# Encoder step on one core: in the first projection, each term's weight tiles start 64 bytes further on than the term's before

## The chip, the cores and the metric

The kernel runs on one core of one Trainium2 chip. Its time is the device time of one execution in microseconds (us); three executions of the kernel before are at hand, and the times of two kernels are compared by their medians. Five engines run their own instruction streams side by side: TensorE (PE in the profile, with its weight loads shown apart as PEld), VectorE (DVE), ScalarE (ACT), GpSimd (POOL) and SyncE (SP, which only issues transfers here).

## The reference

One inference step of a two-layer hybrid encoder, with 2048 prompt tokens and 8 x 16 sample tokens (2176 in all), model width 1024. What matters here is the first line of each layer, the input projection:

```python
def in_proj(x, g, w):
    p = rmsnorm(x, g) @ w
    m = MIX_WIDTH
    return (p[..., :m], p[..., m:2 * m], p[..., 2 * m:3 * m],
            heads(p[..., 3 * m:3 * m + X_WIDTH], H_X, HD_X), p[..., 3 * m + X_WIDTH:])
```

It is a product of a 2176 x 1024 matrix of tokens with a 1024 x 3584 matrix of weights, once for each layer. Layer 0 then does banded softmax attention, layer 1 a gated linear recurrence; both also do a small cross-attention, a gate and an output projection. All tensors are float32.

## The kernel before

The span falls into stages: a short beginning (function `begin`), the first projection (`project` with `l = 0`, from 50.5 us to about 657 us of the profiled execution), banded attention with its output projection (to about 1337 us), the second projection (`project` with `l = 1`, to 1964 us), and the recurrence.

**Seven terms.** A projection is a product of 2 x 2 blocks done with seven block products in place of eight (Strassen's scheme). A pair of 128-column weight groups gives, with its two halves of the 1024 rows, four blocks; `Terms.SUMS` and `Terms.PLAIN` say which sum, difference or plain block is the weight of term j, j = 0 to 6. `Halves` does the same for the tokens. There are 14 pairs (`WPAIRS`), so one pass over all weights has 98 steps (`STEPS`, one step for one term of one pair), and there are four passes (`PASSES`), each over a quarter of the tokens: 320 token columns a term in the first pass (the sample tokens ride along), 256 in the other three. A projection is 392 steps.

**Three products a step.** Each float32 operand is split into a high part in `float32r` and a low part (what the high part leaves out). One step of TensorE is, for each of four 128-row pieces k, three matmuls: weights high with tokens high, weights low with tokens high, weights high with tokens low. That is 12 matmuls a step, each with its own load of a 128 x 128 weight tile. In TensorE's loop:

```python
for i, (a, y) in enumerate(((w.hi, x.hi), (w.lo, x.hi), (w.hi, x.lo))):
    ins = nc.tensor.matmul(BANK[j][:, 0:n], a[j][:, k], x.of(y, p, j)[:, k],
                           start=(k == 0 and i == 0), stop=(k == 3 and i == 2))
```

**Where a term's weights come from.** In the first pass the sums are made from raw weights and kept in DRAM (`tsum`). In the later passes SyncE fetches a term of 256 KB into `pj0_wt` (`Terms.fetch`, once the term's matmuls of seven steps ago are done), ScalarE makes `pj0_wh` from it (`Terms.high`), and VectorE makes `pj0_wl` (`Terms.low`), which lies in the same bytes as `pj0_wt`. TensorE waits for `pj0_wl`. ScalarE and VectorE also take the seven products out of PSUM and combine them into `pj0_out`. Every program order is written out by hand, as loops over the step number `t`; a semaphore count stands for each tile.

**Where the tiles lie.** Tiles are placed one behind the other in each partition of SBUF, in the order in which the code asks for them. By the built program's table of addresses (bytes within a partition): the token tiles `x0_hi` and `x0_lo` of slots 0 to 6 start at 42464 and every 5120 bytes after it, those of slots 7 and 8 at 26080 and every 4096 bytes. A piece k of a token tile is 1280 bytes after the one before it in the first pass, 1024 in the later ones. The weights start at 151072, behind a spacer of 64 bytes (`pj0_shift`): a term is `wh` (2048 bytes) and `wl` (2048 bytes), and its pieces k are 512 bytes apart. So every weight piece that TensorE loads in passes two to four lies 64 bytes above a multiple of 512 bytes away from every token piece. In the first pass a piece k of the tokens is 1280 k bytes on, so that the same figure, the distance modulo 512, is 64 for even k and 320 for odd k. In the second projection, spacers (`pj1_shift0`, `pj1_pad1`, `pj1_shift1`) hold the same 64. In the output projections, the stationary operand is the gated activations and the moving one 512 columns of weights; there the distance modulo 512 is 0 in the odd-numbered jobs of the attention stage, 160 in its even-numbered jobs, and 288 in the recurrence.

What the change touches is `Terms.term`, which places a term's three tiles; it is called in `hybrid_encoder` for j = 0 to 6 of each layer.

Of the kernel before, what the change touches and what calls it, by code (L numbers as in the profile page):

```python
# [20 lines left out]
P = 128  # L21
# [364 lines left out]
class Terms:  # L386
# [22 lines left out]

    def term(self, j, sb, shadowed):  # L410
        l = self.l
        self.hi[j] = sb(f"pj{l}_wh{j}", [P, 4, P], F32R)
        with ExitStack() as shadow:
            self.sum[j] = shadowed(shadow)(f"pj{l}_wt{j}", [P, 4, P])
        self.lo[j] = sb(f"pj{l}_wl{j}", [P, 4, P], F32R)
# [518 lines left out]
def project(nc, l, sem, ps_in, v, x, w, x_of, proj, keep, room, early, samp, opening):  # L934
# [59 lines left out]
    with ExitStack() as ctx:  # L994
# [45 lines left out]
        with nc.Block() as block:  # L1040
# [123 lines left out]
            def _(act):  # L1164
# [56 lines left out]
                for t in range(ALL + 2 * TERMS):  # L1221
# [17 lines left out]
                    if p < PASSES - 1:  # L1239
                        if c in (1, 3, 5, 7) and j == 1:  # L1240
                            square(4 * p + c // 2)
                        if c in (2, 4, 6, 8) and j == 3:
                            evacuate(4 * p + c // 2 - 1, 0)
                        if c in (3, 5, 7, 9) and j == 0:
                            evacuate(4 * p + c // 2 - 1, 1)
                        if (c, j) in ((9, 6), (10, 2)):
                            x.high(nc, act, p + 1, c - 9)
                        for at, term in ((2, 2), (3, 3), (4, 4), (5, 5), (6, 6)):
                            if (c, j) == (WPAIRS - 1, at):
                                act.wait_ge(s_mm, STEPS * (p + 1) - TERMS + term - 1)  # L1250
                                x.high(nc, act, p + 1, term)
# [4 lines left out]
            def _(dve):  # L1256
# [71 lines left out]
                for t in range(ALL + 2 * TERMS):  # L1328
# [20 lines left out]
                    if p < PASSES - 1:  # L1349
                        i = 4 * p + c // 2  # L1350
                        if c in (1, 3, 5, 7) and j == 3:
                            dve.wait_ge(s_sq, i + 1)
                            nc.vector.tensor_scalar(ms[:, i:i + 1], ss[:, i:i + 1], 1.0 / D, EPS, ALU.mult, ALU.add).then_inc(s_ms, 1)
                        if c in (1, 3, 5, 7) and j == 6:
                            dve.wait_ge(s_rs, i + 1)
                            nc.vector.tensor_scalar(nat[i % 2][:], nat[i % 2][:], rs[:, i:i + 1], None, ALU.mult).then_inc(s_xn, 1)
                        for at, term in (((9, 4), 0), ((10, 0), 6), ((10, 5), 2), ((11, 5), 5), ((12, 1), 4)):
                            if (c, j) == at:
                                dve.wait_ge(x.s_raw, RAWS + 8 * (p + 1))
                                if l == 0 and p == 0 and term == 0:  # L1360
                                    dve.wait_ge(keep.s_out, 128)
                                    dve.wait_ge(keep.s_row, 16)
                                x.add(nc, dve, p + 1, term)
                        for at, term in (((10, 2), 0), ((11, 1), 1)):
                            if (c, j) == at:
                                x.low(nc, dve, p + 1, term)
                        for at, term in ((3, 2), (4, 3), (5, 4), (6, 5)):
                            if (c, j) == (WPAIRS - 1, at):
                                x.low(nc, dve, p + 1, term)
# [1973 lines left out]
```

## Time and profile before

| | us |
|---|---|
| median of 3 runs | 2460.17 |
| lowest, highest | 2459.54, 2461.45 |
| the profiled execution's own time | 2456.59 |
| its span, first to last instruction | 2454.8 |
| of that, the first projection's matmuls | 50.5 to 657.1 |

The profiled execution is 3.6 us below the median, and 1.8 us of its own time lies around the span. A row of a view by groups gives, for one line, engine and pair of tiles, the count, the busy time, the mean duration and the idle time before it with what ended it. The distance between the starts of neighbouring matmuls is their price when they are pipelined; the duration of one (some 276 ns) is longer, as it overlaps the next ones.

### The profile page before, as it was taken

The numbers are of one execution on the slowest core, as the hardware profiler recorded it, in microseconds if no ns is written. First come the engines' busy times: TensorE is split into PE (matmuls) and PEld (weight loads), VectorE is DVE, ScalarE is ACT, GpSimd is POOL, SyncE is SP. The second block draws the span as 40 slices with busy tenths as digits, with TensorE's granted clock in tenths as the row PEclk, the third lists the DMA queues.
The fourth block names the chain that finished last, engine by engine and source line by source line (L and its number), as shares of the span: only waits on it lengthen the run. The fifth ranks groups of instructions, "written<-read, shape, count | busy, mean of one in ns | idle before, by whom it ended". The sixth has DMA issues, their size and how long they took to land. (4 is left out here: it accounts for less than half of the span.)

```text
span 2454.8 us, 61024 instructions
## 1 busy us (share of the span) xinstructions
PE 2368.7 (96%) x23677; PEld 2082.7 (85%) x23677; DVE 1852.3 (75%) x3597; ACT 1451.1 (59%) x3323; POOL 372.9 (15%) x585
## 2 busy tenths in 40 slices
PE   7999999999999999999998999999999979999998
PEld 5999999999866777777776899999999978888886
DVE  7899788887665555555555999888898867888885
ACT  4655667755565555454554565676766656666664
POOL 2332000000022111111111332000000031212211
PEclk9999999999999999999999999999999989999999
DMA  6887888889883222222223888888789794344441
GB/s 234 291 288 260 290 284 250 246 260 296 249 261 92 81 79 70 72 76 79 71 78 136 276 291 278 254 264 241 243 253 299 259 285 120 119 139 124 133 139 68
DMA packets 402706, 480.59 MB, mean 196 GB/s; under 512 B 40532, under 2 KB 249228, under 8 KB 402424
## 3 DMA queue, kind: packets, MB, share of 16 engines
q1 hardware_dynamic: 385880, 417.03, 54.5%
q0 software_dynamic: 14704, 54.92, 6.6%
q10 hardware_dynamic: 1840, 4.75, 0.7%
q8 instruction: 192, 3.15, 0.5%
q14 instruction: 90, 0.74, 0.1%
HBM read 329.78 MB, written 151.56 MB: 196 GB/s over the span
## 5 line engine op out<-in xcount | busy, mean ns | idle before, releaser
L1428 PE MATMUL pj_acc<-x_hi,pj_wh 128*128 128x256 f32 (+1 forms) x3080 | 888.9, 289 | 26.4 <-DVE pj_wl L483 23.6
L1428 PE MATMUL pj_acc<-x_hi,pj_wl 128*128 128x256 f32 (+1 forms) x3080 | 876.8, 285 | 0.0
L1428 PE MATMUL pj_acc<-x_lo,pj_wh 128*128 128x256 f32 (+1 forms) x3080 | 876.7, 285 | 0.0
L476 ACT ACTIVATE pj_wh<-pj_wt 128x512 fp32r<-128x512 f32 x718 | 449.8, 634 | 351.5 <-DMA pj_wt<-tsum 245.9
L1428 PEld LDWEIGHTS pj_acc<-x_hi,pj_wh 128*128 128x128 f32 x3080 | 579.0, 188 | 40.2 <-DVE pj_wl L483 37.7
L483 DVE SCALAR_TENSOR_TENSOR pj_wl<-pj_wt,pj_wh 128x512 fp32r<-128x512 f32 x718 | 498.6, 710 | 110.9 <-ACT pj_wh L476 98.9
L1428 PEld LDWEIGHTS pj_acc<-x_lo,pj_wh 128*128 128x128 f32 x3080 | 579.8, 188 | 0.0
L1428 PEld LDWEIGHTS pj_acc<-x_hi,pj_wl 128*128 128x128 f32 x3080 | 579.0, 188 | 0.1
L1275 DVE TENSOR_TENSOR pj_out<-pj_out,pj_acc 128x512 f32<-128x512 f32 (+1 forms) x448 | 320.2, 715 | 66.2 <-PE pj_acc L1428 39.3
L2553 ACT COPY pb_pt<-pb_TP 128x384 f32<-128x384 f32 (+2 forms) x272 | 107.0, 393 | 288.6 <-PE pb_TP L2268 219.4
L2437 DVE COPY pb_pt<-pb_TP 128x256 f32<-128x256 f32 (+2 forms) x266 | 115.8, 435 | 139.8 <-PE pb_TP L2265 130.9
L2420 DVE CUSTOM_DVE_ANT_0 pb_se<-pb_SC,pb_bias 128x640 f32<-128x640 f32 (+4 forms) x204 | 147.9, 725 | 82.4 <-PE pb_SC L2241 75.9
L2265 PE MATMUL pb_TP<-ident,pb_se 128*128 128x128 f32 x1020 | 170.4, 287 | 4.6 <-DVE pb_v L2457 2.7
L2546 ACT ACTIVATE pb_se<-pb_se,pb_mn 128x640 f32<-128x640 f32 (+4 forms) x208 | 156.9, 754 | 8.0 <-DVE pb_mn L2420 3.0
L2265 PEld LDWEIGHTS pb_TP<-ident,pb_se 128*128 128x128 f32 x1020 | 107.2, 140 | 54.5 <-issue 39.7
L2241 PEld LDWEIGHTS pb_SC<-pb_k,pb_q 64*128 64x128 f32 x1128 | 91.1, 186 | 42.2 <-issue 36.6
L2364 PE MATMUL pb_OP<-pb_woh,pb_yh 128*128 128x512 f32 x272 | 119.9, 441 | 2.1 <-DVE pb_x L2487 2.1
L2319 PEld LDWEIGHTS pb_OB<-pb_pt,pb_v 128*64 128x64 f32 x1680 | 89.8, 136 | 34.9 <-ACT pb_pt L2553 26.1
L2241 PE MATMUL pb_SC<-pb_k,pb_q 64*128 64x256 f32 (+1 forms) x1128 | 117.6, 340 | 1.6 <-issue 1.6
L2364 PE MATMUL pb_OP<-pb_woh,pb_yl 128*128 128x512 f32 x272 | 118.5, 436 | 0.0
L2895 PE MATMUL hg_OP<-woh,hg_yh 128*128 128x512 f32 x264 | 116.3, 440 | 0.0
L1175 ACT COPY pj_out<-pj_acc 128x256 f32<-128x256 f32 (+1 forms) x224 | 85.3, 381 | 49.1 <-PE pj_acc L1428 45.8
(354 smaller groups left out, 3922.5 us busy)
## 6 DMA issues: line engine op xcount, KB each, us to landing
pj_wt<-tsum SPq DMA_DIRECT2D x588, 256.0 KB, 3.7
proj<-pj_out SPq DMA_DIRECT2D x112, 512.0 KB, 4.3
tsum<-pj_wt SPq DMA_DIRECT2D x140, 256.0 KB, 3.3
pj_wraw<-in_w_in_dram POOLq DMA_DIRECT2D x24, 1024.0 KB, 7.0
tsum<-pj_wraw SPq DMA_DIRECT2D x56, 256.0 KB, 3.8
hg_x<-x_mid SPq DMA_DIRECT2D x17, 512.0 KB, 3.6
pb_gate<-proj SPq DMA_DIRECT2D x16, 512.0 KB, 5.0
pb_x<-in_x_prompt_dram SPq DMA_DIRECT2D x16, 512.0 KB, 3.5
```

Of the source, the lines that this page charges most:

```text
L476: nc.scalar.mul(self.hi[j][:], self.source(step), scale_of(c, self.l)).then_inc(self.s_hi, 1)
L483: nc.vector.scalar_tensor_tensor(out=self.lo[j][:], in0=self.source(step), scalar=scale_of(c, self.l), in1=self.hi[j][:].bitcast(F32), op0 ...
L1275: nc.vector.tensor_tensor(to, to, what, op).then_inc(s_cb, 1)
L1428: ins = nc.tensor.matmul(BANK[j][:, 0:n], a[j][:, k], x.of(y, p, j)[:, k], start=(k == 0 and i == 0), stop=(k == 3 and i == 2))
L2241: ins = nc.tensor.matmul(SC[h][:, at * P:(at + size) * P], q[T % 2][po:po + HD, p], kring[po:po + HD, p, slot * P:(slot + size) * P], star ...
L2265: ins = nc.tensor.transpose(TP[:, at:at + P], se[u % 2][h][:, i * P:(i + 1) * P], ident[:])
L2364: ins = nc.tensor.matmul(OP[:], (yl if part == 2 else yh)[job % 2][:, k], (wol if part == 1 else woh)[:, group_of(job, k), cs], start=(k = ...
L2420: nc.vector.tensor_tensor_reduce(se[u % 2][h][:, 0:n * P], SC[h][:, 0:n * P], add, 1.0, 3e38, ALU.add, ALU.min, mn[:, at:at + 1]).then_inc ...
L2437: ins = nc.vector.tensor_copy(pt[h][:, low * P:low * P + width], TP[:, 512:512 + width])
L2546: nc.scalar.activation(se[u % 2][h][:, 0:n], src[:, 0:n], ACT.Exp, bias=mn[:, at:at + 1], scale=-1.0, accum_out=tot[:, at:at + 1]).then_in ...
L2553: nc.scalar.copy(pt[h][:, 0:at], TP[:, 0:at]).then_inc(s_eva, 1)
L2895: nc.tensor.matmul(to[:], yh[:, s], woh[:, g, cs], start=(s == 0), stop=False)
```

## The change

One call is added: in the first projection, ahead of the tiles of each term but the first, 16 float32 values (64 bytes in a partition) are left free. Nothing reads or writes them.

```diff
     def term(self, j, sb, shadowed):
         l = self.l
+        if l == 0 and j:
+            sb(f"pj{l}_step{j}", [P, 16])
         self.hi[j] = sb(f"pj{l}_wh{j}", [P, 4, P], F32R)
```

By the two built programs, the instructions of every engine, their order and the semaphores that they wait for are the same; the line numbers behind the edit grow by 2. What differs is the addresses. The tiles of term j lie 64 j bytes further on (`pj0_wh1` 64, `pj0_wh6` 384), and what lies behind them, 384 bytes: the beginning's buffers and `pj0_nat`, `pj0_out`, `pj0_sig`. The distance of term j's weight pieces from the token pieces, modulo 512, becomes 64 (j + 1): 64, 128, 192, 256, 320, 384, 448 in passes two to four. In the first pass it is that for even k, and for odd k 256 bytes on from it (modulo 512): 320, 384, 448, 0, 64, 128, 192. The second projection and the other stages keep their addresses.

## Rows read from the trace of the kernel before

**Rows 1.** The page: busy time by engine, and the costliest groups.

```profile
PE 2368.7 (96%) x23677; PEld 2082.7 (85%) x23677; DVE 1852.3 (75%) x3597; ACT 1451.1 (59%) x3323; POOL 372.9 (15%) x585
...
L1428 PE MATMUL pj_acc<-x_hi,pj_wh 128*128 128x256 f32 (+1 forms) x3080 | 888.9, 289 | 26.4 <-DVE pj_wl L483 23.6
L1428 PE MATMUL pj_acc<-x_hi,pj_wl 128*128 128x256 f32 (+1 forms) x3080 | 876.8, 285 | 0.0
```

**Rows 2.** Busy time and clock in the first projection's four passes, all engines.

```profile
core 0: us, PE busy (x) PEld busy (x) DVE busy (x) ACT busy (x) POOL busy (x), PEclk, DMA share, GB/s
50.50:232.40 181.90, 179.74 (x1208) 177.69 (x1209) 161.40 (x214) 97.82 (x191) 63.32 (x50) 0.99 0.84 279
232.40:374.50 142.10, 140.11 (x1210) 138.41 (x1209) 117.38 (x183) 95.54 (x197) 4.44 (x8) 1.00 0.88 283
374.50:512.70 138.20, 137.51 (x1210) 137.11 (x1209) 117.07 (x183) 96.16 (x196) 7.33 (x7) 1.00 0.80 248
512.70:657.10 144.40, 139.36 (x1178) 137.06 (x1176) 104.33 (x165) 77.27 (x147) 0.00 (x0) 1.00 0.90 270
```

**Rows 3.** Who PE waited for from 50 to 657 us: us, times, longest.

```profile
PE pj_acc L1428 <- DVE pj_wl L483: 8.9, 17, 1.2
```

**Rows 4.** PE in the timeline, from 534 us (fourth pass): start us, duration.

```profile
534.27 0.28 PE L1428 MATMUL pj_acc<-x_lo,pj_wh 128*128 128x256 f32 x1
534.38 0.28 PE L1428 MATMUL pj_acc<-x_hi,pj_wh 128*128 128x256 f32 x1
...
542.43 0.28 PE L1428 MATMUL pj_acc<-x_lo,pj_wh 128*128 128x256 f32 x1
```

**Rows 5.** The same from 617 us (fourth pass).

```profile
617.39 0.28 PE L1428 MATMUL pj_acc<-x_lo,pj_wh 128*128 128x256 f32 x1
617.51 0.28 PE L1428 MATMUL pj_acc<-x_hi,pj_wh 128*128 128x256 f32 x1
...
627.28 0.28 PE L1428 MATMUL pj_acc<-x_lo,pj_wh 128*128 128x256 f32 x1
```

**Rows 6.** Matmuls by group in passes two, three, four, and 542.6 to 570.9 us.

```profile
L1428 PE MATMUL pj_acc<-x_lo,pj_wh 128*128 128x256 f32 x392 | 108.5, 277 | 0.0
...
L1428 PE MATMUL pj_acc<-x_lo,pj_wh 128*128 128x256 f32 x393 | 108.5, 276 | 0.0
...
L1428 PE MATMUL pj_acc<-x_lo,pj_wh 128*128 128x256 f32 x393 | 109.5, 279 | 0.0
...
L1428 PE MATMUL pj_acc<-x_hi,pj_wh 128*128 128x256 f32 x77 | 21.7, 282 | 1.1 <-DVE pj_wl L483 1.1
```

**Rows 7.** First pass: three matmuls at the lower clock, four at the higher.

```profile
53.31 0.47 PE L1428 MATMUL pj_acc<-x_hi,pj_wl 128*128 128x320 f32 x1
53.58 0.47 PE L1428 MATMUL pj_acc<-x_lo,pj_wh 128*128 128x320 f32 x1
...
57.43 0.31 PE L1428 MATMUL pj_acc<-x_hi,pj_wh 128*128 128x320 f32 x1
57.58 0.31 PE L1428 MATMUL pj_acc<-x_hi,pj_wl 128*128 128x320 f32 x1
57.73 0.31 PE L1428 MATMUL pj_acc<-x_lo,pj_wh 128*128 128x320 f32 x1
57.87 0.31 PE L1428 MATMUL pj_acc<-x_hi,pj_wh 128*128 128x320 f32 x1
```

**Rows 8.** Output projections in the timeline: distance 160, 288 and 0, in this order.

```profile
1332.78 0.39 PE L2364 MATMUL pb_OP<-pb_woh,pb_yl 128*128 128x512 f32 x1
...
1334.18 0.39 PE L2364 MATMUL pb_OP<-pb_woh,pb_yl 128*128 128x512 f32 x1
...
2439.77 0.40 PE L2895 MATMUL hg_SC<-woh,hg_yh 128*128 128x512 f32 x1
...
2441.17 0.40 PE L2895 MATMUL hg_OP<-woh,hg_yh 128*128 128x512 f32 x1
...
1028.68 0.40 PE L2364 MATMUL pb_OP<-pb_woh,pb_yh 128*128 128x512 f32 x1
...
1029.14 0.39 PE L2364 MATMUL pb_OP<-pb_woh,pb_yl 128*128 128x512 f32 x1
```

**Rows 9.** VectorE by group: third pass of the first, then of the second projection.

```profile
L1275 DVE TENSOR_TENSOR pj_out<-pj_out,pj_acc 128x512 f32<-128x512 f32 x57 | 38.9, 683 | 11.2 <-PE pj_acc L1428 7.3 <-ACT pj_out L1175 3.9
...
L1275 DVE TENSOR_TENSOR pj_out<-pj_out,pj_acc 128x512 f32<-128x512 f32 x56 | 38.2, 681 | 11.0 <-PE pj_acc L1428 6.8 <-issue 2.4 <-ACT pj_out L1175 1.7
```

## The prediction, made before the changed kernel ran

> **What bounds the kernel now.** I read the page first: TensorE is busy for 96% of the span, and the projections' line 1428 has by far its largest groups [rows 1]. The reader is to see there that no other engine comes near, VectorE being next with 75%. Then the table of the first projection's four passes [rows 2]: TensorE is busy for 139.36 us of 144.40 in the fourth pass and for 137.51 of 138.20 in the third, at a granted clock of 1.00, the higher of its two levels (2.4 GHz). VectorE has 117.07 us of the third pass's 138.20 (85%), the DMA engines 80 to 90% of each pass. Waits are few: in all of the first projection TensorE stood still for `pj_wl` for 8.9 us in 17 waits [rows 3]. So what bounds this stage is how closely TensorE's matmuls follow each other, and the change can only act there: by the front part no instruction, order or wait differs, only addresses.
>
> Then I read the spacing, matmul by matmul, in the fourth pass. It has two values. In a narrow stretch 72 matmuls of 256 columns start within 542.43 - 534.27 = 8.16 us, 113.3 ns each [rows 4]. In a wide stretch 84 start within 627.28 - 617.39 = 9.89 us, 117.7 ns each [rows 5]. The tiles are of the same kinds, the clock is the same, and the distance between weights and tokens, modulo 512 bytes, is 64 in both. A stretch keeps its value over all seven terms until TensorE next stands still. The wide one costs 117.7 - 113.3 = 4.4 ns a matmul. How much of a pass is slow can be read from the mean duration, which is 281 to 282 ns where all spacings are wide and 276 where none is [rows 6]: the second pass has 277, the third 276, the fourth 279. So the wide share is about 1/5, 0 and 3/5 of the 1176 matmuls of a pass, some 900 of 3528, or with the rounding of the means 600 to 1100.
>
> 256 columns at 2.4 GHz would be 106.7 ns, so even the narrow value has 6.6 ns on top. The first pass's 320 columns (133.3 ns by the clock) come every 146.7 ns: the three gaps from 57.43 to 57.87 are 0.15, 0.15 and 0.14 us [rows 7]. At the lower clock, 1.2 GHz, they come every 0.27 us, and 320/1.2 is 266.7 ns: nothing on top. Something that feeds TensorE is a little too slow at the full clock, and the question is whether the distance of the two operands has a hand in it.
>
> **The change part by part.** (1) The new distances in passes two to four: 3528 matmuls, of which 6/7, 3024, get another distance. What a distance of 128 to 448 costs no row of this projection shows, so I bound it. From below: all of the 6.6 ns go, 3528 x 6.6 = 23 us less (and the wide stretches' 600 to 1100 x 4.4 = 3 to 5 us with it). From above: every matmul gets the wide spacing that has the narrow one now, 3528 - 900 = 2630 x 4.4 = 11.6 us more. Between them I take zero, by the rows nearest in kind. In the first pass the distance is 64 for even k and 320 for odd k, and the gap from the second to the third and fourth of its matmuls does not follow k: 0.15, 0.15, 0.14 [rows 7], the first three being of one k and the fourth of the next. In the output projections, six matmuls of 512 columns take 1334.18 - 1332.78 = 1.40 us at distance 160, and six take 2441.17 - 2439.77 = 1.40 us at distance 288: 233.3 ns both. At distance 0 two take 0.46 us, 230 ns, with an error of some 5 ns [rows 8]. Four different distances show no price that I can tell from zero, while one distance, 64, shows two prices. The spacing is then not made by the distance alone.
>
> (2) The first pass: 1176 matmuls at 146.7 ns, with distances that now run through 0 to 448. Bounds: 13.4 ns less each, 15.8 us, if all the excess went; 4.4 ns more each, 5.2 us, if a second, wider spacing like that of 256 columns exists there, of which the trace shows nothing. I take zero, by the same rows.
>
> (3) Where the wide stretches begin and end. Each begins after a wait of TensorE for `pj_wl`, and each stretch runs on over terms whose distance is the same. With another distance at each step, the spacing may be drawn anew at each of the 294 steps. If it never holds, the 600 to 1100 wide spacings become narrow: 3 to 5 us less. If it is drawn as often as now, zero. I take zero, since no row shows what ends a stretch but a wait. A part of any such gain would be eaten up: the wide spacing stands mostly in the fourth pass, whose DMA share is 0.90 [rows 2], and there TensorE waits for terms that land late.
>
> (4) The 384 bytes by which `pj0_out`, `pj0_nat` and `pj0_sig` move, and the weights' own 64 bytes for ScalarE, VectorE and the transfers: zero. The second projection has its tiles at wholly other addresses, and the combining of `pj_out` takes 681 ns there against 683 here [rows 9]. VectorE's cover for it would be 15% of a pass. (5) The beginning's buffers move by 384 bytes with all else alike: zero for the same reason.
>
> The sum is 0 on the profiled execution's 2456.59 us. That lies 3.6 us under the median of 2460.17, so the forecast stands at 2460.2 us.
>
> On one point a page can be weighed against these rows. The Trainium skill, page "SBUF — State Buffer", section "A bandwidth-pool intuition that's wrong (but worth ruling out)", gives TensorE's weight loads a second, independent read port beside that of the moving operand. By that rule no distance could matter, the sum would be exactly zero and every rival below but the first would fall. The trace agrees in that the rows at four distances show one price, and does not bear the rule out in full, as some unnamed thing costs 113.3 - 106.7 = 6.6 ns a matmul.
>
> **The rivals.** *The wide spacing is broken up.* For it speaks that a wide stretch holds its spacing over hundreds of matmuls [rows 5], as two streams would that run at a fixed offset, and that offset now changes at each step. Against it: the narrow stretch at the same distance is just as lasting. It gives 3 to 5 us less, 2455 to 2457. That is mostly inside 0.2%, the bound of what a measurement of this kernel can tell from no change (4.9 us).
>
> *Some distances are bad ones.* The mechanism: weight loads and moving reads of one matmul run at the same time and meet in one part of the memory when their distance is a multiple of 128 or 256 bytes. The old 64, 320, 160 and 288 never are; 128, 256 and 384 (terms 1, 3 and 5) are. Those three terms are 3/7 of 3528, 1512 matmuls; if all were wide and the rest as often as now (900 x 4/7 = 514), the wide ones grow from 900 to 2026, and 1126 x 4.4 = 5.0 us, 2465. If each distance above 64 were bad, 11.6 us, 2472, and with the first pass up to 2477. It decides, passing 4.9 us, when 1110 matmuls more are wide, a third of the three passes. Against it speaks distance 0, the worst one by this mechanism, with 230 ns where the others have 233.3 [rows 8]; but those are two matmuls at a time, of another width.
>
> *A wider distance feeds better.* The excess of 6.6 and 13.4 ns falls for some terms. If three of seven lost it, 23 x 3/7 + 15.8 x 3/7 = 17 us less, 2443; in full, 2421, though the DMA engines, at 80 to 90%, would take back a part as late terms. Against it: 64 and 320 in the first pass behave alike, and 160 and 288 do.
>
> *The change does nothing at all*, since only the distance modulo 64 bytes counts, which is untouched. That gives the forecast's time, and I count it in.
>
> **How the numbers follow.** Zero by whatever reason, with a point either way of 2 us: 0.36. The wide spacing broken up: 0.17, of which 0.04 beyond 4.9 us. Bad distances: 0.30, of which 0.05 stay within 4.9 us. A wider distance feeds better: 0.17, of which 0.02 within. That makes 0.19 for faster, 0.56 for the same (0.36 + 0.13 + 0.05 + 0.02), and 0.25 for slower. For 8 in 10 the range takes in the slower rival up to 2472 and of the faster one what is less than 14 us: 2446 to 2472.
>
> **What would show it.** In the profile after, the mean duration of the 256-column matmuls by pass (276 or 277, 276 and 279 before) and the spacing in steady stretches. If I am right, they are 113.3 and 117.7 ns for every term, and wide stretches still begin only behind waits. If terms 1, 3 and 5 alone have 117.7 ns or more, the second rival holds. If a wide stretch ends at a step's edge without a wait, the first does. A spacing under 113 ns in any term, or under 146 in the first pass, is the third. The second projection, at unchanged addresses, should keep its time; if it moves as much as the first, the difference is the execution's and not the change's. I am wrong if the first projection's four passes together, 606.6 us, change by more than 5 us.

## The result: slower by 0.3%, and where the time went

The changed kernel takes 2467.07 us (median of 20 runs, 2462.6 to 2471.94), the kernel before 2459.96 us (20 runs beside them, 2452.76 to 2466.79). The ratio is 1.0029, with a 95% interval of 1.002 to 1.0038: 7.1 us slower.

The first view is again the table of the first projection's four passes, now of the changed kernel. Columns are the stretch, its length, then busy time and count of PE, PEld, DVE, ACT and POOL, the granted clock, the DMA share and GB/s:

```profile
core 0: us, PE busy (x) PEld busy (x) DVE busy (x) ACT busy (x) POOL busy (x), PEclk, DMA share, GB/s
50.90:235.00 184.10, 180.09 (x1209) 177.53 (x1210) 161.91 (x214) 97.73 (x191) 61.78 (x50) 0.99 0.84 276
235.00:380.80 145.80, 144.15 (x1211) 142.61 (x1210) 117.67 (x184) 96.27 (x197) 4.44 (x8) 1.00 0.86 276
380.80:524.00 143.20, 142.75 (x1210) 142.14 (x1209) 117.48 (x183) 96.61 (x197) 7.33 (x7) 1.00 0.78 239
524.00:667.30 143.30, 141.58 (x1178) 139.23 (x1176) 103.99 (x164) 76.49 (x146) 0.00 (x0) 1.00 0.91 272
```

Against [rows 2] the third pass is 5.0 us longer (143.2 against 138.2) with the same clock, the same counts on every engine to within one, and the same work on VectorE (117.5 against 117.1 us). The second is 3.7 us longer, the fourth 1.1 us shorter. Passes two to four together take 432.3 us against 424.7, and the four together 616.4 against 606.6. The first pass, 2.2 us longer, kept its spacing. What grew in it is the time that TensorE waited for `pj_wl`, from 1.8 us (four waits, the longest 1.0) to 3.5 us (four, the longest 2.0). No run shows whether the change brought that on.

The matmul groups of the second, third and fourth pass, in this order, name the cause:

```profile
L1430 PE MATMUL pj_acc<-x_lo,pj_wh 128*128 128x256 f32 x392 | 109.8, 280 | 0.0
...
L1430 PE MATMUL pj_acc<-x_lo,pj_wh 128*128 128x256 f32 x393 | 110.1, 280 | 0.0
...
L1430 PE MATMUL pj_acc<-x_lo,pj_wh 128*128 128x256 f32 x393 | 110.1, 280 | 0.0
```

The mean duration is 280 ns in all three, where it was 277, 276 and 279 [rows 6]: the wide spacing has become the rule. The timeline shows it term by term. These are the first matmuls of seven steps in a row (terms 0 to 6 of one pair of the fourth pass) and of the step behind them:

```profile
647.49 0.28 PE L1430 MATMUL pj_acc<-x_hi,pj_wh 128*128 128x256 f32 x1
...
648.86 0.28 PE L1430 MATMUL pj_acc<-x_hi,pj_wh 128*128 128x256 f32 x1
...
650.27 0.28 PE L1430 MATMUL pj_acc<-x_hi,pj_wh 128*128 128x256 f32 x1
...
651.69 0.28 PE L1430 MATMUL pj_acc<-x_hi,pj_wh 128*128 128x256 f32 x1
...
653.13 0.28 PE L1430 MATMUL pj_acc<-x_hi,pj_wh 128*128 128x256 f32 x1
...
654.50 0.28 PE L1430 MATMUL pj_acc<-x_hi,pj_wh 128*128 128x256 f32 x1
...
655.92 0.28 PE L1430 MATMUL pj_acc<-x_hi,pj_wh 128*128 128x256 f32 x1
...
657.34 0.28 PE L1430 MATMUL pj_acc<-x_hi,pj_wh 128*128 128x256 f32 x1
```

The steps last 1.37, 1.41, 1.42, 1.44, 1.37, 1.42 and 1.42 us. Terms 0 and 4 go at 1.37/12 = 114 ns, the others at 118 to 120. A mean over all of passes two to four takes each term's 42 steps, and of each step only the gaps from the fourth to the last, so that the start behind a wait stays out. These means are 115.5, 119.1, 117.9, 119.4, 115.3, 119.2 and 117.9 ns for terms 0 to 6. Before, each term had 114.1 to 114.4 ns.

The means follow the distances. The distances of terms 0 to 6 are 64, 128, 192, 256, 320, 384 and 448 bytes. Terms 0 and 4, 1 and 5, 2 and 6 agree, and they are 256 bytes apart. The rest of this text calls the distance modulo 256 the place, and a step wide when its matmuls are over 116 ns apart. Place 64 has 113.3 or 117.9 ns, as before, and the others are wide in every step.

What the wider spacing costs is partly given back. The means add up to 24.4 ns more over the seven terms, and 24.4 x 42 x 12 = 12.3 us. The three passes got only 7.6 us longer. Of who PE waited for in them, before and after:

```profile
PE pj_acc L1428 <- DVE pj_wl L483: 7.1, 13, 1.2
```

```profile
PE pj_acc L1430 <- DVE pj_wl L485: 3.5, 12, 0.8
```

TensorE waited 3.6 us less for the next term's weights. That it used them up more slowly is the likely reason: the runs below fit it, with 3.1 to 5.0 us of such waits in e2, e7, e8 and e9, whose terms are mostly or all wide, and 6.1 and 7.2 us in e1 and e4, whose terms are at 64.

The second projection, with its addresses unchanged, is a check on the profiled execution itself. The same view of it, before and after:

```profile
1376.00:1964.00 588.00, 571.00 (x4633) 563.13 (x4632) 512.56 (x780) 386.55 (x763) 59.06 (x55) 1.00 0.83 266
```

```profile
1384.70:1968.90 584.20, 568.60 (x4634) 561.09 (x4632) 513.19 (x781) 387.48 (x763) 58.59 (x55) 1.00 0.84 268
```

It fell by 3.8 us by itself, its passes two to four alone by 5.7 us (427.2 to 421.5). Its terms' means were 113.8 to 114.2 ns before and are 113.3 to 113.6 now, which means fewer wide steps. So part of the first projection's 9.8 us is hidden in the two profiled spans (2461.0 against 2454.8 us), and such shifts may be a good part of the scatter between runs of one kernel, 14 us in the 20 of before. They also say how far a stretch's length in one trace can be trusted: in the traces of this text that leave the second projection at place 64, its passes two to four took 421 to 428 us. That is why the argument below rests on the spacing of the steps first, and on lengths only where they leave that band.

### The profile page after: what moved, and what is told of

It reads as the page before. It is cut to its first block and busy times, and to the rows that moved or that the text cites. A ratio compares the mean times of both kernels' runs of the same rounds, so it can differ in the third digit from the quotient of the medians.

```text
span 2461.0 us, 61024 instructions
## 1 busy us (share of the span) xinstructions
PE 2378.4 (97%) x23677; PEld 2091.8 (85%) x23677; DVE 1853.2 (75%) x3597; ACT 1452.4 (59%) x3323; POOL 370.8 (15%) x585
## 5 line engine op out<-in xcount | busy, mean ns | idle before, releaser
L2366 PE MATMUL pb_OP<-pb_woh,pb_yh 128*128 128x512 f32 x272 | 119.2, 438 | 2.1 <-DVE pb_x L2489 2.0
L2243 PE MATMUL pb_SC<-pb_k,pb_q 64*128 64x256 f32 (+1 forms) x1128 | 117.5, 340 | 0.9 <-issue 0.9
L2366 PE MATMUL pb_OP<-pb_woh,pb_yl 128*128 128x512 f32 x272 | 117.9, 433 | 0.0
L2897 PE MATMUL hg_OP<-woh,hg_yh 128*128 128x512 f32 x264 | 116.2, 440 | 0.0
```

The source lines that it names most:

```text
L2243: ins = nc.tensor.matmul(SC[h][:, at * P:(at + size) * P], q[T % 2][po:po + HD, p], kring[po:po + HD, p, slot * P:(slot + size) * P], star ...
L2366: ins = nc.tensor.matmul(OP[:], (yl if part == 2 else yh)[job % 2][:, k], (wol if part == 1 else woh)[:, group_of(job, k), cs], start=(k = ...
L2897: nc.tensor.matmul(to[:], yh[:, s], woh[:, g, cs], start=(s == 0), stop=False)
```

## The experiments

Theory R: the spacing of these matmuls depends on the place, that is the distance between the weight tile and the token tile modulo 256 bytes. Its rivals: theory S, what disturbs is that the distance changes from one term to the next; theory A, the tiles' own addresses count. The edits are shown in part, against the kernel before where nothing else is said. A ratio and its interval are those on record, and they can differ a little from the quotient of the two medians beside them.

### Other distances, the same place

```diff
     def term(self, j, sb, shadowed):
         l = self.l
+        if l == 0 and j in (1, 4):
+            sb(f"pj{l}_step{j}", [P, 64])
```

> Weights of terms 1 to 3 lie 256 bytes further on, of terms 4 to 6 512 bytes, so the distance to the tokens takes the values 64, 320, 576 and is always 64 modulo 256. Theory R (the spacing depends on the distance modulo 256, read from the changed kernel: residue 64 gives 113.3 or 117.9 ns, 128 gives 118.9, 192 gives 117.9, 0 gives 120.3): as the kernel before, 2460 us within 4, passes two to four of the first projection about 425 us, spacings of 113.3 and 117.9 ns alone. Theory S (any change of the distance from term to term disturbs the stream): as the changed kernel, 2467 us, passes two to four about 432 us.

Measured: 2462.28 us against 2462.48 beside it, ratio 1.0005 (0.9993 to 1.0018). Passes two to four:

```profile
232.10:660.40 428.30, 420.64 (x3594) 414.95 (x3592) 339.01 (x529) 268.29 (x538) 11.79 (x15) 1.00 0.85 265
```

428.3 us lies between the two theories' figures, but the steps decide: all seven terms have means of 114.6 to 114.9 ns and only the two spacings 113.3 and 117.9, with 12 to 15 wide steps of 42 in each (7 to 10 before). Steps in the distance do no harm as long as the place stays. That speaks against S, and the next run, which loses without any step in the distance, rules it out as the cause.

### All terms at place 128

```diff
-                sb0("pj0_shift", [P, 16])
+                sb0("pj0_shift", [P, 32])
```

> All seven terms lie 128 bytes above a multiple of 512 from the tokens, none steps. Theory R: 118.9 ns for each of the 3528 matmuls of passes two to four instead of a mean of 114.3, 16 us more, 2476 us, passes two to four about 440 us. Theory S: nothing steps, so as before or a little better, 2460 us or less.

Measured: 2470.17 us against 2462.48, ratio 1.0022 (1.0005 to 1.0038). Passes two to four:

```profile
232.30:669.30 437.00, 431.64 (x3593) 428.33 (x3592) 339.00 (x529) 270.07 (x538) 11.77 (x15) 1.00 0.84 259
```

The first matmuls of a step, of the next, and of the step six further on:

```profile
409.55 0.28 PE L1428 MATMUL pj_acc<-x_hi,pj_wh 128*128 128x256 f32 x1
...
410.98 0.28 PE L1428 MATMUL pj_acc<-x_hi,pj_wh 128*128 128x256 f32 x1
...
419.52 0.28 PE L1428 MATMUL pj_acc<-x_hi,pj_wh 128*128 128x256 f32 x1
```

Seven steps take 9.97 us, so 9.97/84 = 118.7 ns a matmul with nothing stepping. The three passes take 12.3 us more than before, where R said 16 and S said none. Not all of that is the place. At 622.7 us TensorE waited 2.04 us for `pj_wl`, and soon behind this wait it ran for 3.4 us at the lower of its two clock levels, its matmuls 213 ns apart, which the rounded 1.00 above hides:

```profile
626.00:629.50 3.50, 3.50 (x19) 3.50 (x19) 2.58 (x5) 1.19 (x3) 0.00 (x0) 0.52 0.87 201
```

By the count of these matmuls, some 18 at 213 ns in place of 118.6, this cost about 1.7 us (an estimate), so some 10.6 us are left. The whole kernel became only 7.7 us longer than the runs beside it, with a wide interval (some 1 to 9 us).

### The same place 128, made by moving the tokens

```diff
                 x = Halves(nc, sem, 0)
+                sb0("x0_shift", [P, 48])
...
                 x.raws(sb0, sb_in)
+                sb0("pj0_back", [P, 16])
                 w = Terms(sem, 0, w_in, tsum)
```

> The tokens are moved by 192 bytes and the weights by 256, so the distance is 128 modulo 256 while the weights' own address stays what it was modulo 256. Theory R (the distance counts): as e2, 118.6 ns in passes two to four, which last about 437 us. If the weights' own address counts: as before, 113.3 and 117.9 ns, about 425 us.

```profile
232.30:669.00 436.70, 432.34 (x3593) 428.42 (x3592) 338.53 (x529) 268.90 (x538) 11.76 (x15) 1.00 0.86 260
```

436.7 us against e2's 437.0, with the same dip of the clock at 626 us in both. Outside it all seven terms have 118.6 to 118.8 ns. The weights' own address modulo 256 is that of the kernel before, and still the loss is there in full. The kernel took 2470.95 us (one run).

### Both moved by 32 bytes

```diff
                 x = Halves(nc, sem, 0)
+                sb0("x0_shift", [P, 8])
```

> Tokens and weights alike lie 32 bytes further on, so that every one of them starts at a multiple of 64 bytes; the distance stays at 64. Theory R: 113.3 and 117.9 ns as before, passes two to four about 425 us within 5. Theory A (the tiles' own addresses count): another spacing, perhaps less than 113.3 ns if starting at a multiple of 64 helps.

```profile
234.20:660.80 426.60, 418.99 (x3594) 413.92 (x3592) 338.49 (x529) 269.10 (x538) 11.78 (x15) 1.00 0.85 265
```

Means of 114.2 to 114.7 ns and 426.6 us, as before. The kernel took 2467.13 us (one run), more than expected but inside the 2457.43 to 2472.87 of the kernel before beside it. With the last two runs, A falls and R stands: the distance counts, and neither operand's own address explains the loss.

### A grid of 32 bytes

The spacer ahead of the first term is 32 bytes, and each further term steps by 64, as in the changed kernel.

```diff
-                sb0("pj0_shift", [P, 16])
+                sb0("pj0_shift", [P, 8])
...
+        if l == 0 and j:
+            sb(f"pj{l}_step{j}", [P, 16])
```

> Distances 32, 96, 160, 224, 288, 352, 416 for terms 0 to 6. Theory R: terms 0 and 4, 1 and 5, 2 and 6 have the same spacing pair by pair, since they agree modulo 256; what the values are it does not say, but one may be under 113.3 ns. Theory S: no pairs, all terms between 117 and 120 ns.

The first matmuls of the steps of terms 0 to 4 of one pair:

```profile
412.00 0.29 PE L1430 MATMUL pj_acc<-x_hi,pj_wh 128*128 128x256 f32 x1
...
413.43 0.28 PE L1430 MATMUL pj_acc<-x_hi,pj_wh 128*128 128x256 f32 x1
...
414.86 0.28 PE L1430 MATMUL pj_acc<-x_hi,pj_wh 128*128 128x256 f32 x1
...
416.29 0.28 PE L1430 MATMUL pj_acc<-x_hi,pj_wh 128*128 128x256 f32 x1
...
417.69 0.28 PE L1430 MATMUL pj_acc<-x_hi,pj_wh 128*128 128x256 f32 x1
```

These steps last 1.43 us at places 32, 96 and 160, and 1.40 at 224. The pairs that R asks for are there: 118.3 and 118.3 ns (terms 0 and 4), 118.6 and 118.9 (1 and 5), 120.0 and 120.0 (2 and 6). Of the eight places on this grid, 64 is the best, and 224 with a steady 116.7 ns the next. The kernel took 2473.72 us (one run).

### Finer grids

The terms' tiles are cut out of one wide tile, so that they can start at any multiple of 4 bytes. In `Terms`:

```diff
+    AT = (40, 48, 56, 60, 68, 72, 80)
+
+    def at(self, whole, j, part):
+        a = 2 * j * 4 * P + self.AT[j] // 4 + part * (4 * P + 0)
+        return whole[:, a:a + 4 * P].rearrange("p (k n) -> p k n", k=4)
```

> Distances of terms 0 to 6 modulo 256: 40, 48, 56, 60, 68, 72, 80, all near the 64 of before. In e3 32 gave 118.3 and 96 gave 118.9 ns, before 64 gave 113.3 or 117.9. Theory R narrow: only a few bytes around 64 give 113.3, the others 118 to 119. Theory R broad: the offset in time between two reads counts, so the spacing falls gradually towards 64 and several of the seven show 113.3. Theory blocks of 64 bytes: 40 to 60 read as 32 did (118.3), 68 to 80 as 64 did (113.3 or 117.9).

The means of terms 0 to 6 are 119.1, 118.0, 117.7, 120.0, 118.3, 118.2 and 118.7 ns. At 60 and 68, 4 bytes beside 64, every step is wide, and neither blocks of 64 bytes nor a slow fall towards 64 can be seen. The narrow form of R holds. 2475.43 us (one run).

Two more kernels differ in `AT` alone: (176, 208, 216, 232, 240, 248, 272) and (24, 52, 88, 104, 112, 144, 200).

> Distances of terms 0 to 6 modulo 256: 176, 208, 216, 232, 240, 248, 16. In e3 224 gave 116.7 ns throughout, 160 gave 120.0, and the changed kernel 192 gave 117.9. Theory R: each term has its own spacing, 208 to 232 between 116.7 and 117.9, and 240, 248 and 16 rise towards the 120 of residue 0. If one of them is at or under 113.3 ns in every step, it beats the 64 of before, which has 117.9 in a part of its steps.

> Seven more distances modulo 256, for terms 0 to 6: 24, 52, 88, 104, 112, 144, 200. By theory R in its narrow form each has its own steady spacing between 116.7 and 120 ns, and 64 stays alone at 113.3; should one of them show 113.3 or less in every step, a better place than 64 exists. In the first pass (320 columns) the spacing should lie between 144.5 (seen at 48) and 150 ns (seen at 60).

The first gave 117.9, 116.8, 119.7, 117.6, 119.8, 118.4 and 118.3 ns, nothing better than 64. The second gave 119.1, **114.8, 114.0**, 120.0, 119.5, 118.4 and 121.3 (the last two, places 144 and 200, without one step each that a dip of the clock at 628 us made longer): the places 52 and 88 come down to 113.3 ns within a step. Place 200 has 123 ns in most of its steps and 117 in others, so 64 is not alone in having two spacings. Its terms 1, 2 and 3 of one pair in the timeline:

```profile
434.39 0.40 PE L1442 MATMUL pj_acc<-x_hi,pj_w 128*128 128x256 f32 x2
...
435.78 0.39 PE L1442 MATMUL pj_acc<-x_hi,pj_w 128*128 128x256 f32 x2
...
437.15 0.40 PE L1442 MATMUL pj_acc<-x_hi,pj_w 128*128 128x256 f32 x2
```

Term 1 (place 52) lasts 1.39 us, its later gaps being 113 and 114 ns; term 2 (place 88) lasts 1.37. So R's claim that 64 is alone was wrong, and my guess for the first pass (144.5 to 150 ns by place) too: there all seven had 146.7 to 147.1. The whole kernels took 2465.48 and 2475.41 us (one run each).

### Only the low parts at a bad place

All seven high parts lie one behind the other at place 64, all low parts behind them at 128. The wide tile is cut with

```diff
+        a = 16 + (part * TERMS + j) * 4 * P + 16 * part
```

> The high parts of the weights stay at distance 64 (modulo 256) from the tokens, the low parts lie at 128. A low part is loaded while the first of the three matmuls runs and a high part while the second and third run. If what counts is the tile being loaded against the tokens being streamed at that moment, the matmul of high weights and high tokens gets wide (118 to 120 ns) and the two others may keep 113.3, a mean near 115.5. If one bad distance spoils the whole sequence: 118 ns or more in all three.

```profile
238.40:674.50 436.10, 430.21 (x3593) 425.76 (x3592) 339.71 (x529) 268.08 (x538) 11.77 (x15) 1.00 0.84 260
```

All seven terms have 118.1 or 118.2 ns, and the passes take 436.1 us. By product, the next matmul starts 119.5 ns after that of high weights and high tokens, 116.2 after low weights and high tokens, and 119.0 after high weights and low tokens, on average. A third of the weight loads at a bad place costs about as much as all of them, and all three products pay. The idea that each matmul pays for its own pair of tiles, with 113.3 ns in two of three, fell. 2475.81 us (one run).

### The change in both projections

The edit is against the changed kernel.

```diff
-        if l == 0 and j:
+        if j:
             sb(f"pj{l}_step{j}", [P, 16])
```

> The change is made in the second projection too, so its terms' distances run through 64, 128, ... 448 as in the first. Theory R: the second projection goes the way of the first, its last three passes get some 7 to 10 us longer (427 to about 436 us), and the whole takes twice the change's 7.1 us, 2474 us (ratio 1.004 to 1.008). If the loss belongs to what is special to the first projection (its buffers' other moves, the load of cached keys in its last pass): the time of the changed kernel, 2467 us, ratio 1.003.

Measured: 2475.61 us against 2457.25, ratio 1.0064 (1.0041 to 1.0087), about twice the change's 1.0029. Passes two to four of the first and of the second projection:

```profile
233.90:666.80 432.90, 428.63 (x3594) 424.02 (x3592) 338.99 (x529) 270.07 (x538) 11.77 (x15) 1.00 0.84 262
1549.70:1985.90 436.20, 429.14 (x3594) 424.31 (x3592) 359.11 (x578) 293.84 (x582) 7.81 (x14) 1.00 0.82 253
```

The second one's 436.2 us stands against 427.2 before (1536.8 to 1964.0 us), outside the band of 421 to 428. Its terms have 115.5, 119.1, 117.7, 119.4, 115.7, 119.2 and 117.9 ns: to 0.4 ns the list of the first projection. So the loss needs nothing that is special to the first projection, such as its buffers or its load of cached keys.

### Places 52 and 88, a try to beat both kernels

All terms of the first projection lie at place 52, all of the second at 88, cut out of wide tiles by a new function `group`. The edit of the first projection:

```diff
-                sb0("pj0_shift", [P, 16])
-                for j in range(TERMS):
-                    w.term(j, sb0, sb_in)
+                sb0("pj0_shift", [P, 8])
+                w.group(range(TERMS), 5, sb0, sb_in)
```

> All terms of the first projection at distance 52 modulo 256, all of the second at 88: the two places where e10, each in one term of seven, came down to 113.3 ns within eight matmuls. If they do so by themselves, whatever the stream did before, both projections lose the 117.9 ns that 64 has in a part of its steps: some 800 matmuls by 4.4 ns in each, 3 to 7 us off the whole, 2453 to 2457 against 2460, and passes two to four of each projection within a few us of 420. If what came down in e10 was owed to the terms beside them, spacings of 117 to 120 ns remain and the time is 2460 to 2480 us.

Measured: 2466.21 us against 2461.09, ratio 1.0016 (1.0003 to 1.0029). In the timeline, the first matmuls of two steps of the first projection that lie seven steps apart, and of two such steps of the second:

```profile
410.99 0.39 PE L1431 MATMUL pj_acc<-x_hi,pj_w 128*128 128x256 f32 x2
...
420.50 0.28 PE L1431 MATMUL pj_acc<-x_hi,pj_w 128*128 128x256 f32 x1
...
1723.55 0.39 PE L1431 MATMUL pj_acc<-x_hi,pj_w 128*128 128x256 f32 x2
...
1733.07 0.39 PE L1431 MATMUL pj_acc<-x_hi,pj_w 128*128 128x256 f32 x2
```

Passes two to four of both projections:

```profile
233.10:664.50 431.40, 420.19 (x3594) 413.64 (x3592) 339.26 (x529) 268.23 (x538) 11.79 (x15) 1.00 0.85 263
1548.00:1971.50 423.50, 415.41 (x3593) 411.13 (x3591) 359.32 (x578) 292.20 (x582) 7.83 (x14) 1.00 0.83 260
```

What PE waited for in those of the first:

```profile
PE pj_acc L1431 <- DVE pj_w L488: 10.2, 24, 0.9
```

Seven steps in 9.51 and 9.52 us are 113.3 ns at both places. But neither place holds it always: wide steps remain, 4 to 14 of 42 in a term at 52, where place 64 had 7 to 10 before, and 4 to 7 at 88, where place 64 had 4 to 7 before in the same projection. The wide steps mostly have 117.5 ns at 52 (some 120.1) and 116.6 at 88. And the first projection's passes take 431.4 us, with 24 waits for the next term's weights of 10.2 us in all, where the kernel before had 13 of 7.1. The gain of 3 to 7 us that I expected did not come. Why there are more waits at place 52 wasn't tried; the transfers of a term land in 4.1 us against 3.9 before, and whether the tiles' start at a multiple of 4 bytes alone has a part in that is open.

## Why the prediction was right or wrong

**Right:** what bounds the stage. In passes two to four only TensorE's spacing and its waits moved, at the same clock and counts. The price of a wide matmul at place 64, 4.4 ns, and its two values, 113.3 and 117.7 to 117.9, came back in every run with tiles at 64. The first pass kept its spacing, as part 2 said. Part 4 (buffers moved by 384 bytes cost nothing) is borne out as far as VectorE shows it, 117.5 against 117.1 us in the third pass, and e1 moved the same buffers by 512 bytes at no loss that can be told from none. Part 5 was not tested by itself.

**Luck:** the time. The measured 2467.07 us lies in the range of 2446 to 2472, but the range reached that far only for a rival. The spacing cost 12.3 us in passes two to four, more than the 11.6 of part 1's upper bound, and a part of it came back as fewer waits, for which the range was not drawn. By the prediction's own sign it was wrong: the four passes changed by 9.8 us, and 5 was the limit. The second projection moved by 3.8 us the other way, which shows that such a sign, taken from one trace, has an error of that size. The steps do not, since no term at place 64 was ever wide in all 42.

**Wrong:** the forecast of no change. Its chance was 0.56 against 0.25 for slower. The step that failed is part 1, "Four different distances show no price that I can tell from zero". The rows were read as saying more than they could. In the first pass, 64 and 320 differ by 256 bytes: they are the same place, so I had compared a thing with itself. Also the 320-column matmuls feel the place far less: in the changed kernel, whose first pass runs through all four places of its grid, steady steps keep 146.5 to 146.7 ns, and only three of the finer places showed much else (144.2 at 48, 144.4 at 248, 150.0 at 60). The output projections' 512 columns were a third width, and their rows could not tell what 256 columns do. None of my rows had both this width and another place, and the right reading would have been "unknown, between -23 and +11.6 us", not zero. Part 1 measured +12.3 us. That this is over its upper bound is a matter of size: the matmuls that were wide before, read as 900 from mean durations, were 59 steps of 294, some 710 matmuls.

Part 3 had a premise wrong as well, that each wide stretch begins after a wait for `pj_wl`. In the kernel before, one begins at 266.45 us and one at 591.69 us behind matmuls that are 149 and 214 ns apart, with no such wait:

```profile
591.58 0.28 PE L1428 MATMUL pj_acc<-x_lo,pj_wh 128*128 128x256 f32 x1
591.69 0.38 PE L1428 MATMUL pj_acc<-x_hi,pj_wh 128*128 128x256 f32 x1
591.90 0.29 PE L1428 MATMUL pj_acc<-x_hi,pj_wl 128*128 128x256 f32 x1
```

**The rivals.** *Some distances are bad ones* is what happened, with the wrong rule. The rival took multiples of 128 bytes for bad and 192 and 448 for good, with 1126 matmuls more at 4.4 ns and 2465 us. Its mechanism, two reads that meet in one part of the memory, was not tested. In fact five terms of seven are bad, at 4.6 to 6.1 ns over 113.3, and even place 64 was wide in 20 and 18 of 42 steps (7 and 8 before), which makes 12.3 us. The waits gave back 3.6 us of it, a term that the rival's sum lacked, though part 3 named it for a gain. *The wide spacing is broken up* was right in its mechanism: at 647.49 and 653.13 us a step of 114 ns begins right behind wide ones with no wait between. It was of no use, since the spacing that follows in five terms of seven is worse. *A wider distance feeds better*: with 256 columns no place of 29 gave less than 113.3 ns. With 320 columns places 48 and 248 did gain, 144.2 and 144.4 ns against 146.6 to 146.8 at 64, but the changed kernel has neither. *Nothing at all, since only the distance modulo 64 counts*: false, 4 bytes count.

**The page.** The Trainium skill's "SBUF — State Buffer", in "A bandwidth-pool intuition that's wrong (but worth ruling out)", gives the weight loads an independent port, by which no distance could matter. The trace does not agree. By addresses alone e2 and e7 widened all seven terms to 118.6 ns and more and made the three passes 12 us longer, dip of the clock included, and the measurement decides.

## What to carry to other kernels

A change that moves only addresses can cost 0.3%: look at the starts of the matmuls, one after the other, before and after, since mean durations (280 ns against 276 to 279) all but hide a spacing that is 4% wider. Before rows of other cases are taken as neighbours of an unknown price, ask whether they differ from the known case in the thing that counts, and in that alone. And a few ns a matmul won or lost come back only in part, as fewer or more waits for the next tiles.

## What the runs showed of the hardware

- The spacing of float32r matmuls with 256 moving columns, 12 a step with a new weight tile each, depends on the distance between weight and token tiles modulo 256 bytes, down to single words: at 2.4 GHz 113.3 ns at 64 bytes and 120.0 at 60.
- Of 29 places, three (52, 64, 88) reach 113.3 ns, and there a second spacing exists beside it: 117.9 ns at 64, mostly 117.5 at 52 and 116.6 at 88. At 64, where all terms lie there, the spacing changes from one to the other only at a gap of 128 ns or more, mostly of over 200. At 52 and 88 up to twelve wide matmuls behind an interruption also pass into the narrow spacing by themselves (in e11 at 351 us with no gap over 120 ns, at 1556.5 us with none over 126). The other places have means between 116.7 and 120.0 ns, and 121.3 at 200. What chooses the spacing at one place isn't settled.
- With one product of three at another place, all three are wide (e8: 119.5, 116.2 and 119.0 ns).
- With 320 moving columns the spacing depends on the place far less: 146.4 to 147.2 ns at most places, 144.2 at 48, 144.4 at 248 and 150.0 at 60.
- It isn't shown which part of the chip makes the spacing depend on the distance.
